# First block of a fused transformer kernel on one Trainium2 core: three moves in the order of its small steps around the q heads and the start of the output projection

## The reference, cut to what matters

```python
ada = jax.nn.silu(c) @ w_ada[l] + b_ada[l]                      # 6 x 2048 modulation values
h = modulate(rmsnorm(x, norm1_g[l]), sh1, sc1)
q, k, v, qi, ki, wi, p = jnp.split(h @ w_in[l], offsets, axis=-1)
qi, ki = rope_partial(qi...), rope_partial(ki...)               # index queries (16 heads), one index key head
score = einsum('bths,bth->bts', relu(einsum(qi, ki)), wi)       # index scores
_, sel = lax.top_k(score, n_sel)                                # 64 keys per query
attn_out = softmax attention of 8 heads over the selected keys
pool_out = multiscale_pool(p, w_pool[l], pool_scale[l])
mix = jnp.concatenate([attn_out, pool_out], axis=-1) @ w_out[l]
x = x + gt1 * mix
x = x + gt2 * hier_moe(h2, ...)                                 # 32 experts, top 2 of one group
```

## Time and profile before

| | |
|---|---|
| median of 3 runs | 2313.37 us (2312.64 to 2315.13) |
| profiled execution | 2312.69 us, of it span 2310.9 us |
| TensorE busy | 2070.4 us, 90% |
| VectorE busy | 1248.6 us, 54% |
| ScalarE busy | 868.1 us, 38% |
| DMA queue | 693.78 MB, 77.8% of 16 engines |
| granted TensorE clock, mean | 0.987 |

### The profile page before, as it was taken

One profiled execution on the slowest core, in us unless ns is written; L12 is line 12 of the kernel. 1 busy time (PEld: TensorE's weight loads), 2 busy tenths in 40 slices (PEclk: granted clock), 3 DMA queues, 4 the chain that ended last, 5 costly groups with the idle time before them and its releaser, 6 DMA issues.

```text
span 2310.9 us, 38449 instructions
## 1 busy us (share of the span) xinstructions
PE 2070.4 (90%) x14546; PEld 1350.6 (58%) x14546; DVE 1248.6 (54%) x2271; ACT 868.1 (38%) x1329; POOL 55.0 (2%) x56
## 2 busy tenths in 40 slices
PE   6899998998988888888888888899999999999998
PEld 2677767772222222222222222799899999998898
DVE  3455567545444444444444444677766554468655
ACT  3343344431211111111111111567756544466654
POOL 0000000000000000000000000110100000011000
PEclk9999999999999999999999999899999999999999
DMA  9998876889999999999999999554445555543443
GB/s 373 366 350 302 311 285 243 293 337 404 427 427 428 427 428 427 428 427 427 428 428 427 427 427 427 198 175 147 141 146 183 176 177 185 178 157 119 142 126 112
DMA packets 121943, 695.42 MB, mean 301 GB/s; under 512 B 13536, under 2 KB 13664, under 8 KB 60384
## 3 DMA queue, kind: packets, MB, share of 16 engines
q1 hardware_dynamic: 121824, 693.78, 77.8%
HBM read 691.63 MB, written 2.10 MB: 300 GB/s over the span
## 4 chain that ended last, share of the span: by engine, by line
PE 45%; DMA 34%; DVE 10%; ACT 5%; SPq 3%; issue 3%; DVEq 0%; ACTq 0%
DMA ring<-in_w 30%; PE acc L1289 29%; DVE WL L2045 3%; PE psO L1348 3%; DMA land<-in_stream_a 3%; PE psS L1557 3%; PE acc L1286 3%; ACT WH L1726 2%; SPq L1103 2%; DMA land<-in_stream_bc 1%; PE acc L1156 1%; PE psM L1156 1%; PE psO L1228 1%; DVE HL L2058 1%; DVE X L2200 1%
## 5 line engine op out<-in xcount | busy, mean ns | idle before, releaser
L2045 DVE TENSOR_TENSOR WL<-land,WH 128x1024 fp32r<-128x1024 f32 (+2 forms) x346 | 416.9, 1206 | 396.1 <-ACT WH L1726 391.8
L1289 PE MATMUL acc<-HH,WH 128*128 128x256 f32 x2000 | 586.2, 293 | 4.2 <-DVE HL L2064 2.2
L1289 PE MATMUL acc<-HH,WL 128*128 128x256 f32 x2000 | 568.9, 284 | 0.0
L1289 PE MATMUL acc<-HL,WH 128*128 128x256 f32 x2000 | 568.5, 284 | 0.0
L1726 ACT ACTIVATE WH<-land 128x1024 fp32r<-128x1024 f32 (+2 forms) x350 | 362.5, 1037 | 207.7 <-PE acc L1289 151.8
L1289 PEld LDWEIGHTS acc<-HH,WH 128*128 128x128 f32 x2000 | 386.8, 193 | 26.5 <-issue 12.6
L1289 PEld LDWEIGHTS acc<-HH,WL 128*128 128x128 f32 x2000 | 387.1, 194 | 2.6 <-issue 2.0
L1289 PEld LDWEIGHTS acc<-HL,WH 128*128 128x128 f32 x2000 | 386.5, 193 | 0.0
L1557 PE MATMUL psS<-ring,low 128*32 128x512 f32 x2048 | 272.6, 604 | 102.3 <-DMA ring<-in_w 100.6
L1557 PEld LDWEIGHTS psS<-ring,low 128*32 128x32 f32 x2048 | 40.7, 108 | 312.7 <-DMA ring<-in_w 284.8
L1887 ACT ACT_TABLE_LOAD x32 | 41.1, 1283 | 442.1 <-PE psS L1557 442.1
(11 more groups left out here) (425 smaller groups left out, 2611.7 us busy)
## 6 DMA issues: line engine op xcount, KB each, us to landing
ring<-in_w SPq DMA_DIRECT2D x384, 1024.0 KB, 26.0
land<-in_stream_bc SPq DMA_DIRECT2D x246, 512.0 KB, 4.1
land<-in_stream_a SPq DMA_DIRECT2D x92, 1024.0 KB, 8.0
land<-in_stream_a SPq DMA_DIRECT2D x100, 512.0 KB, 6.6
land<-in_stream_bc SPq DMA_DIRECT2D x12, 384.0 KB, 3.7
X<-in_xT SPq DMA_DIRECT2D x1, 2048.0 KB, 15.7
out<-low SPq DMA_DIRECT2D x3, 512.0 KB, 2.7
cst<-in_const SPq DMA_DIRECT2D x1, 1514.5 KB, 10.4
```

The costliest lines, as they stand in the source:

```text
L1289: mm = pe.matmul(bank[:, 0:S], w[:, kk, :], h[rows[kk]], start=(z == 0 and i == 0), stop=stop)
L2045: ins = dve.tensor_tensor(wl, src, wh, ALU.subtract)
```

## The change

The index keys' rotation ("rot", ("kw", 0)) is put on the list `misc`, so it uses psM and no longer psT. The last step of the q heads, ("q", 7), no longer issues a load, an index step or a ranking part: the mix split of chunks 8 to 15, the load of half 61, an index step and the ranking part 3 follow it, in that order, and a last index step comes before each remaining ada group. The turn of ada 16 moves behind ("wp", 0). And ("T", 0) waits for VectorE's end of the last ada turn that used psT (16), where it waited for that of the last turn before it of any bank (17).

```diff
@@ -349,7 +349,7 @@
     def rotate(self, x):
         self.add("pe", "rot", x)
         if x[0] != "qr":
-            (self.early if x[0] in ("k", "kw", "qi", "q") else self.misc).append(("rot", x))
+            (self.early if x[0] in ("k", "qi", "q") else self.misc).append(("rot", x))
         self.add("dve", "rot", x)
 
 
@@ -516,7 +516,8 @@
         return step if x[0] == "q" else (lambda: between(ADA_RATE[2])) if x[0] == "qi" else between
 
     for x, post in rest:
-        o.proj(x, post=post, between=halfway(x))
+        final = x == ("q", 7)
+        o.proj(x, post=post, between=halfway(x), loads=0 if final else 1)
         if x in pool_at:
             o.add("dve", "pool", *pool_at[x])
         if x in pmm_at:
@@ -525,18 +526,20 @@
                 o.add("pe", *item)
                 o.acc.append(item)
                 o.add("act", "evac", item)
-        if x[0] == "q" and x[1]:
+        if x[0] == "q" and x[1] and not final:
             index()
-        if x[0] == "q" and x[1] >= 4:
+        if x[0] == "q" and 4 <= x[1] < 7:
             topk(0, x[1] - 4)
     o.split_mix("wo", 2, 3)
     ada(*left.pop(0))
+    o.load()
     index()
+    topk(0, 3)
     while len(left) % 4:
         ada(*left.pop(0))
-    index()
+        if idx:
+            index()
     assert not idx
-    ada_t(23 - len(left) // 4)
     shared[0], owed[0] = True, 0.0
 
     def after():
@@ -545,6 +548,7 @@
     for n in range(KD):
         o.proj(("wp", n), halves=[o.halves_of["wo", n][0]], post="res", between=after if 0 < n < 14 else None)
         if n == 0:
+            ada_t(23 - len(left) // 4)
             o.add("dve", "qrms")
             o.add("act", "qsqrt")
             o.add("dve", "qrec")
@@ -1210,7 +1214,8 @@
                     if k == 0 and n == 0:
 
                         needs(k, "dve", o, *o.early[-1])
-                        needs(k, "dve", o, "adaT", max(s[1] for s in o.steps["pe"][:o.at["pe"][("T", 0)]] if s[0] == "adaT"))
+                        turned = [s[1] for s in o.steps["pe"][:o.at["pe"][("T", 0)]] if s[0] == "adaT" and s[1] not in o.small_bank]
+                        needs(k, "dve", o, "adaT", turned[-1])
                     needs(k, "dve", o, "scale", j)
                     if n:
                         needs(k, "act", o, "pt", jobs[n - 1])
```

## The result

| | before, beside it | changed | ratio, 95% interval |
|---|---|---|---|
| first comparison | 2314.25 (4 executions) | 2295.99 (4; 2294.48 to 2300.67) | 0.9929 [0.9914, 0.9945] |
| c1_after_again | 2311.13 (17) | 2299.21 (6; 2295.50 to 2305.34) | 0.9950 [0.9933, 0.9966] |
| c3_after_more | 2311.26 (11) | 2299.13 (6; 2294.67 to 2302.16) | 0.9939 [0.9922, 0.9956] |

The medians are in us. The changed kernel is faster by 18.3, 11.9 and 12.1 us in the three comparisons. All 16 executions of it have the median 2298.8. The forecast gain of 11.75 us is a ratio of 0.9949: it lies inside the intervals of the two later comparisons and outside that of the first. The profiled execution of the first comparison has a span of 2292.7 us, where before had 2310.9.

What follows compares the result with a forecast made beforehand. TensorE bounds the first block except at three standstills, with VectorE the bound between the last two; DMA feeds the expert phase. Gains of 2.9 + 8.85 = 11.75 us give 2301.6 us, range 2299.8 to 2306.0.

Steps and rivals of the forecast that it cites:

- Part 1: Index keys' rotation in psM: TensorE's 2.83 us wait at the second rotation goes, a gain of 2.9 us.
- Part 2: Mix split ahead of the ranking, adaT 16 behind ("wp", 0): VectorE reaches qrms 3.7 us earlier and stays so.
- The delayed load of stream_a: SP's load needs half 61 freed, at 337.2; ("ada", 17, 1) keeps a margin of 5.4 us, so no cost.
- a wait for stream_a behind 345: Sign of being wrong: a wait for stream_a showing up after 345 us in the changed profile.
- Part 3: (T, 0) waits for adaT 16 only: ("ada", 18, 0) starts 8.85 us earlier, 5.15 of them from this part.
- (a): Rival: the clock falls again around (T, 0), about 1 us is lost, 2302.6; chance 0.15.
- full clock behind its waits: TensorE's waits of 0.8, about 2 and 1.3 us counted at full clock, nearest row being the 2.83 us wait.
- (b): Rival: the index keys' 2.9 us is given back before 331 by a late transfer, 2304.5; 0.15 including other losses.
- (c): Rival: the stream sets the first block's end, shrinking the shift, in the extreme to none, 2313.4; 0.05 for within 0.2%.
- (d): Rival: SP's load behind half 61 makes TensorE wait for ("ada", 17, 1); slower, 2318 if free at 359.4; chance 0.03.
- The sum: 2.9 us at the index keys plus 8.85 us at ("ada", 18, 0) make 11.75 us, giving 2301.6.
- Nothing makes it much faster: Under range and chances: VectorE's queue holds the rest of what TensorE could gain, so the range starts at 2299.8.

Runs made afterwards that it cites:

- c1_after_again: The changed kernel with no edit, run again beside before; 2299.21 us (6 executions), ratio 0.9950.
- c3_after_more: The changed kernel with no edit, run for more executions; 2299.13 us (6 executions), ratio 0.9939.
- e1: The kernel before with only the index keys' rotation moved to psM; 2308.82 us, ratio 0.9983.
- k1: The kernel before with unused matmuls filling TensorE's waits ahead of the turn of ada 16 and the first turn of attention weights; 2306.57 us, ratio 0.9981.
- c2: The kernel before with no edit, one more look; 2311.96 us in its one execution.
- e2: The changed kernel with the index keys' bank and the wait of (T, 0) set back, leaving the new order around the last q head; 2309.10 us, ratio 0.9983.
- e5: The changed kernel with qrms ahead of q7's rotation and adaT 16, and a ranking part of the second half later; 2298.33 us, ratio 0.9943.
- e6: e5 with VectorE's softmax preparation of job 0 moved ahead of the ranking part (1, 2); 2297.20 us, ratio 0.9932.
- e3: The kernel before with only the wait of the first turn of attention weights changed; 2306.06 us, ratio 0.9972.

## Why the prediction was right, and where it was off

**Part 1** was forecast at 2.9 us; the distance from the first rotation to the turn of adaT 16 shows 3.1 in e1. That the clock does not fall behind a wait of 2.83 us was true of the trace it was read from and not of k1's.

**Part 2** came step by step: the index wait 0.84 us (0.8 forecast), the wait for qrms 2.11 (about 2), 3.69 us of gain at qrms (3.7). The delayed load of stream_a cost nothing visible at ("ada", 17, 1). A DMA wait of 0.48 us at 353.46 is in the one profile, not in those of c1 and c3, whose distance is the same. The forecast had named a wait for stream_a behind 345 as a sign of being wrong. It is none here: the kernel before has such a wait at the same group in its c2 profile (0.70 us).

**Part 3** as well: (T, 0) waited 0.87, 1.42 and 1.44 us for the scale in the three profiles (1.3), ("ada", 18, 0) 0.62, 0.61 and 0.62 for adaT 17 (0.7).

**The rivals.** (a) did not occur: the granted clock is 1.00 over 300 to 380 us in all three profiles, with the turns of (T, 0) at 0.63 us. So here a wait of 1.4 us with turns on both sides did not bring the clock down. The Trainium skill ("TensorE: Matmul & The Clock Gate", "Part 4: PE-mode transpose") says that transposes do not count as busy TensorE as matmuls do; by these traces that, if so, cost nothing at this place. But the forecast counted full clock behind its waits because the clock had stayed up after one wait of 2.83 us, and that argument doesn't hold: behind 2.83 us the clock fell in k1, and behind 2.09 us, the changed kernel's own wait for qrms, in e2. That it stayed full in all three profiles of the changed kernel owes something to luck: of the four profiles with the wait of 2.1 us, it fell in one. (b) did not occur, and (c) not to any size: the gain at shiftW is 11.9 us, and the expert phase begins 84.5, 84.5 and 83.5 us behind it, before 83.9, 83.7 and 83.7, so at most 0.8 us of it was given back there. (d) did not occur.

**The sum** is right at the edited places: 11.75 us forecast, 11.9 at shiftW, 11.9 and 12.1 in the two larger comparisons.

**The step that failed** is the one under range and chances: "Nothing makes it much faster", and with it the lower end of 2299.8. The first four executions had the median 2295.99, and all 16 have 2298.8. Two things were left out. The first is the base. The sum was taken from one profiled execution and a median of three that lay within 2.5 us, at 2313.37. In the later comparisons the kernel before has medians of 2312.62 (35 executions), 2311.13 (17) and 2311.26 (11); 11.75 off the last two gives 2299.4 and 2299.5, which c1 and c3 hit within 0.4 us. (These three groups ran on three chips, 1, 4 and 3; whether the chip sets the base was not tried.) In the first comparison the base is no excuse: before had 2314.25 beside it, which less 11.75 is 2302.5, 6.5 us above what was measured. The second is the scatter of executions: one unchanged kernel ran from 2307.24 to 2319.05, and the changed one from 2294.48 to 2305.34. A median of four can be 3 us off, and two of the first four were at 2294.5. The range had terms for costs and none for this. Of the first profile's lead beyond the 12 us, 4.3 us lie ahead of the first rotation and 2.5 in the experts and the second block, where nothing was edited.

Where the scatter arises, the marks show: in the stretch ahead of the first rotation, 169.7 to 175.9 us long, and in the one from the expert phase to the end, 1785.2 to 1788.9 us long in the six profiles of the two kernels. The second was not followed up. For the first stretch, the windows of the first profile of the changed kernel

```profile
60.00:120.00 60.00, 53.28 (x399) 38.54 (x399) 29.36 (x43) 21.99 (x27) 0.00 (x0) 0.94 0.98 392
120.00:176.00 56.00, 53.94 (x427) 46.09 (x426) 32.60 (x47) 24.18 (x36) 0.00 (x0) 1.00 0.89 334
```

against c3's

```profile
60.00:120.00 60.00, 53.14 (x386) 38.44 (x387) 29.79 (x44) 21.85 (x28) 0.00 (x0) 0.91 0.98 389
120.00:176.00 56.00, 52.35 (x399) 43.46 (x398) 28.44 (x41) 23.34 (x35) 0.00 (x0) 0.97 0.88 330
```

and c2's

```profile
60.00:120.00 60.00, 49.78 (x376) 36.57 (x380) 29.99 (x47) 22.80 (x30) 0.00 (x0) 0.94 0.94 363
120.00:176.00 56.00, 53.63 (x421) 44.00 (x421) 29.01 (x42) 22.46 (x34) 0.00 (x0) 1.00 0.92 347
```

show two different losses: c3 has nearly the bytes (389 GB/s against 392) and a lower clock, c2 the clock and fewer bytes (363). Why an execution gets fewer bytes there was not tried. It also stays open whether the changed kernel is worth 1 or 2 us beyond the 12. The first comparison says so, the later two and the marks don't; a clock fall behind the index keys' wait, which part 1 rules out, would be such a gain, seen in one profile of six.

## What to carry to other kernels

Measure an edit by the distance between two marks in the trace that enclose it: in the three profiles each of before and of the changed kernel it repeats within 0.3 us, while the whole time of the kernel before spreads over 12. But one such distance can still hold a low clock that another execution doesn't have (1.8 us in e1, 1.4 in k1), so check the granted clock between the marks. A forecast of a time needs the spread of executions in its range, and three runs do not show it. Where two engines feed each other, work taken off the one that looks like the bound gives little (e5: 0.4 us) until the small step that the other one waits for is moved to the front (e6: 2.1 us more).

## What was unexpected of the hardware

The clock behind one and the same standstill differs between executions. After 2.83 us of idle TensorE it stayed at full in five profiles and fell to 0.62 for 3.7 us in the sixth (k1). After some 2.1 us ahead of ("ada", 17, 0) it stayed at full in the three profiles of the changed kernel and fell to 0.57 for 4.0 us in e2. After 4.4 us it fell in all five profiles with this wait, but the work behind it, 3.34 us at full clock, took 4.75 us in one of them (e3) and 6.01 in another (e1).
